# Thirty-two unused bytes ahead of the modulation columns, in a two-block forward pass on one core

## The reference

```python
# first block, twice (layer 0: short convolution; layer 1: latent attention, 8 heads)
x = layer_norm(ALPHA * x + mixer(x))            # mixer: projections, conv or attention, projection back
x = layer_norm(ALPHA * x + square(relu(x @ w1)) @ w2)      # w1: 1024 x 4096, w2: 4096 x 1024
# second block, twice (layer 0: gated linear recurrence; layer 1: block attention)
shift, scale, gate = split(silu(c) @ mod_w + mod_b, 3)
h = rms_norm(x) * (1 + scale) + shift
x = x + gate * mixer(h)
return rms_norm(x)
```

## Time and profile before

| what | value |
|---|---|
| median of 3 runs | 780.79 us (780.48, 780.79 and one of 935.18) |
| span of the profiled execution, first to last instruction | 778.4 us |
| TensorE matmuls in it | 4982, busy 768.9 us |
| VectorE, ScalarE, GpSimd busy | 586.1, 405.1 and 34.6 us |
| TensorE clock granted, mean over the span | 0.998 of full speed |
| read from memory | 172.10 MB, 222 GB/s over the span |

### The profile page before, as it was taken

The page is one execution under the profiler, slowest core; times in us unless marked ns, Lnnn a source line. Parts: engine busy times, 40 slices in busy tenths (PEclk is TensorE's granted clock), DMA queues, the critical chain, the costliest instruction groups (busy, mean ns, idle before and its releaser), DMA issues.

```text
span 778.4 us, 12084 instructions
## 1 busy us (share of the span) xinstructions
PE 768.9 (99%) x4982; PEld 697.1 (90%) x4982; DVE 586.1 (75%) x786; ACT 405.1 (52%) x512; POOL 34.6 (4%) x66
## 2 busy tenths in 40 slices
PE   9999999999999999999999999999999999999996
PEld 9999888988998889888889988998799988999995
DVE  5886898868688697687989776676687877756754
ACT  5455235545445424875355444445649869664632
POOL 0000000000000001000000000000500051000001
PEclk9999999999999999999999999999999999999999
DMA  9877438897867731446488977876235254754102
GB/s 351 319 274 278 184 125 324 348 320 289 313 231 288 290 122 62 163 139 267 165 326 344 347 273 275 308 263 245 103 109 216 109 216 163 270 216 164 55 3 80
DMA packets 26983, 173.94 MB, mean 223 GB/s; under 512 B 3248, under 2 KB 3632, under 8 KB 7856
## 3 DMA queue, kind: packets, MB, share of 16 engines
q1 hardware_dynamic: 26640, 173.14, 60.0%
q10 hardware_dynamic: 288, 0.02, 0.0%
HBM read 172.10 MB, written 1.05 MB: 222 GB/s over the span
## 4 chain that ended last, share of the span: by engine, by line
PE 93%; DVE 3%; ACT 2%; POOL 1%; issue 0%; POOLq 0%; ACTq 0%
PE bank L578 12%; PE bank L580 12%; PE bank L579 12%; PE Y L714 10%; PE Y L716 10%; PE Y L713 10%; PE bank L1067 2%; PE bank L1068 2%; PE bank L1069 2%; PE bank L996 2%; DVE w_low L1610 1%; PE bank L816 1%; PE Y L738 1%; PE bank L610 1%; PE bank L619 1%; PE bank L611 1%
## 5 line engine op out<-in xcount | busy, mean ns | idle before, releaser
L1610 DVE TENSOR_TENSOR w_low<-raw,w_high 128x2048 fp32r<-128x2048 f32 (+3 forms) x125 | 278.5, 2238 | 65.1 <-ACT w_high L1203 62.8
L1203 ACT CAST w_high<-raw 128x2048 fp32r<-128x2048 f32 (+3 forms) x125 | 232.5, 1869 | 92.9 <-DMA raw<-weights 80.0
L578 PE MATMUL bank<-xT_h,w_high 128*128 128x256 f32 x728 | 206.5, 284 | 0.1
L579 PE MATMUL bank<-xT_l,w_high 128*128 128x256 f32 x728 | 205.8, 283 | 0.0
L580 PE MATMUL bank<-xT_h,w_low 128*128 128x256 f32 x728 | 205.8, 283 | 0.0
L578 PEld LDWEIGHTS bank<-xT_h,w_high 128*128 128x128 f32 x728 | 139.4, 192 | 1.6 <-DVE w_low L1610 0.3
L579 PEld LDWEIGHTS bank<-xT_l,w_high 128*128 128x128 f32 x728 | 139.4, 191 | 1.1
L580 PEld LDWEIGHTS bank<-xT_h,w_low 128*128 128x128 f32 x728 | 139.5, 192 | 0.0
L714 PE MATMUL Y<-w_low,hT_h 128*128 128x512 f32 x324 | 128.3, 396 | 0.0
L713 PE MATMUL Y<-w_high,hT_h 128*128 128x512 f32 x324 | 128.0, 395 | 0.0
L716 PE MATMUL Y<-w_high,hT_l 128*128 128x512 f32 x324 | 101.9, 395 | 0.0
(11 more groups left out here) (291 smaller groups left out, 1144.5 us busy)
## 6 DMA issues: line engine op xcount, KB each, us to landing
raw<-weights SPq DMA_DIRECT2D x149, 1024.0 KB, 5.0
rows<-rows_in SPq DMA_DIRECT2D x9, 512.0 KB, 7.7
raw<-weights SPq DMA_DIRECT2D x4, 576.0 KB, 3.5
z<-gates_in SPq DMA_DIRECT2D x4, 512.0 KB, 3.8
raw<-weights SPq DMA_DIRECT2D x2, 896.0 KB, 4.4
raw<-weights SPq DMA_DIRECT2D x3, 512.0 KB, 7.0
x<-x_in SPq DMA_DIRECT2D x2, 512.0 KB, 4.4
kT<-rows_in SPq DMA_DIRECT2D x2, 512.0 KB, 8.3
```

Of the source, the lines that this page charges most:

```text
L578: mm(dst, high, xh[:, kt, :], start=kt == 0, stop=False)
L579: mm(dst, high, xl[:, kt, :], start=False, stop=False)
L1203: nc.scalar.copy(w_high[:, n % RING, start:COLS[n]], raw[:, s % RAW, start:COLS[n]]).then_inc(w_high_ready, 1)
L1610: tt(w_low[:, n % RING, start:COLS[n]], slot[:, start:COLS[n]], f32(w_high[:, n % RING, start:COLS[n]]), ALU.subtract).then_inc(raw_done, 1)
```

## The change

One tile of 128 x 8 float32 (32 bytes in each partition) is declared between `cols` and `modcol`. Nothing reads or writes it. No instruction is added, removed or moved; nine tiles move up by 32 bytes: `modcol`, `buf_a`, `buf_b`, `hT_h`, `hT_l`, `kT`, `area`, `small` and `prm`. `hT_h` then starts at byte 197,440, 64 past a multiple of 128, and `hT_l` at 203,584, the same.

```diff
@@ -294,6 +294,7 @@
         consts = sb("consts", [P, 2 * P + 2 * SEQ])
         ones = sb("ones", [P, P])
         cols = sb("cols", [P, NCOL])
+        sb("space_0", [P, 8])
         modcol = sb("modcol", [P, 2 * NMOD])
         buf_a = sb("buf_a", [P, 2, 512])
         buf_b = sb("buf_b", [P, 2, 512])
```

## The result

The changed kernel takes 774.95 us (median of 5 runs, 774.49 to 775.68), the kernel before 780.49 (median of 5 runs, one of which took 935.18). The ratio is 0.9931, with a 95% interval of 0.9918 to 0.9943: 5.5 us faster, and clear of noise, though well under 2%. The profiled execution took 774.49 us, the least of the five, and its span is 772.7; before it was 778.4. One unused line moves every line number behind it up by one: L713, L714, L716 of before are L714, L715, L717 here.

What follows compares the result with a forecast made beforehand. TensorE, busy for 768.9 of 778.4 us, was taken to bound the kernel. The span of 778.4 less 6.6 plus 0.8 gives 772.6, and with 2.4 us outside it 775.0; 8-in-10 range 773.2 to 781.6 us.

Steps and rivals of the forecast that it cites:

- What bounds the kernel: Whole kernel: TensorE, busy 768.9 of 778.4 us, waits for nothing long; distances between matmul starts make the time.
- What is removed: 996 matmuls with hT stationary, in down and the latents' values: each start 6.7 ns earlier, 6.6 us saved.
- the low end of 5.7: The same 996 matmuls with hT stationary, judged by record durations: 5.7 ns each, 5.7 us saved.
- second rival: Lines longer than 64 bytes make hT's new place worse: 6.6 us slower, 787.4 us, or 788 with hT moving; chance 0.07.
- What the moving side adds: 444 matmuls in mo and mla with hT moving: 0.8 us slower if the 3 and 1 ns are the address's.
- The tiles set at nothing: The other moved tiles, such as area, kT and buf_b, on TensorE, ScalarE and VectorE: no gain.
- The bound for the chain's parts on other engines: VectorE's and ScalarE's 3% and 2% of the chain: a few ns an instruction, below 0.1 us.
- First rival: The 32 bytes aren't the cause of the 6.7 ns, so no change: 780.8 us, or 781.6 with hT moving; chance 0.16.
- The rule of on-chip memory in lines of 16 bytes: Old and new hT addresses are multiples of 16, so the address change would do nothing; objection to the forecast.
- the fetch in whole lines: Fetching hT as stationary operand loses the line's part ahead of the tile: 32 bytes cost 6.7 ns a matmul.
- my reading of the 6.7 ns: hT's extra per matmul over xT as 8 lost elements at 0.83 ns, suggesting a 64-byte line.
- Third rival: Only half of hT's stationary excess is the address: 3.0 us less 0.8 won, 778.6 us; chance 0.05.

Runs made afterwards that it cites:

- the fastest kernel: Against the kernel before, padding puts xT 192 bytes, hT_h 0 and hT_l 192 from the weights' start, modulo 256: 765.57 us, ratio 0.9807.
- At 0: Against the kernel before, 96 unused bytes behind cols in place of the change's 32, so hT, like xT, is 0 from the weights modulo 256: 776.16 us.
- both at 192: Against the changed kernel, xT also moved, so xT and hT start 192 bytes from the weights' start modulo 256: 765.68 us, ratio 0.9818.

## Why the prediction was right, and where it wasn't

The predicted 775.0 us was met, within 0.1, and the mechanism was right in kind: the address of `hT` sets the distances on a full TensorE. That the number is so close is luck. Two of its terms were off in opposite directions, by 2.5 and 2.0 us, and 0.6 us more came from a start that the change isn't shown to touch. There was a fourth error: the median run has 1.8 us outside its span (774.95 to 773.2), not the 2.4 that the prediction added, and its span is 0.5 us longer than that of the profiled execution.

- What bounds the kernel: right. TensorE is busy for 99% after as before, and its waits are as few; new is one of 0.2 us for `x` at the start. The gain in a step (5.60 + 5.74 to 5.50 + 5.76) reached the end undiminished. No supply of weights came due, not even in the fastest kernel, whose step is 10.99 us and whose only wait for weights is one of 0.2 us, as before. The clock "at the top level throughout" was read from a row that doesn't show the slow distances of the first 26 matmuls.
- "What is removed", 6.6 us: mis-sized, 4.1 measured, and below the low end of 5.7. The step that failed is the one that took `xT` as the model of a tile at 64 past a multiple of 128. It isn't: `hT` went from 233.3 to 229.0 ns and not to 226.7. (The matmuls are 1002 and not 996; six in mo were overlooked, worth 0.03 us.) The second rival had named that gap and drawn the wrong conclusion from it.
- "What the moving side adds", 0.8 us: the wrong sign, 1.2 us won. I had the rows for it and read them as saying that a misaligned moving tile is a little faster and an aligned one as slow as `xT`. At 0 it is so (1.9 us more than in the changed kernel, 0.7 more than before); r = 192 is a third case.
- The tiles set at nothing: right within 0.9 us. The bound for the chain's parts on other engines was worked out too small: VectorE's 3% of the chain is 23 us, some 34 instructions, and 7 ns off each would be 0.2 us and not "below 0.1". The 0.6 us at the start had no term.
- First rival, no change: fell, by the kernel that moves only `hT`. Its point that plain float32 doesn't show the effect stays true: `kT` by `z` has records of 379 ns in all 14 traces, and starts 216 ns apart. The rule of on-chip memory in lines of 16 bytes (the Trainium skill, "SBUF — State Buffer", section "Specifications (TRN2)") doesn't decide here: every place tried is a multiple of 32, hence of 16, and `hT` stationary goes from 227 to 234 ns.
- Second rival, a line of 128: fell. So did the fetch in whole lines on which it and my reading of the 6.7 ns rested: moving the weights alone, from a multiple of 128 to 64 past one, made the matmuls with `xT` moving faster, and a lost part of a line could only have made them slower.
- Third rival, half: on the stationary side nearer than I gave it, which won 4.3 of 6.7 ns, though not by one line of `down` and not the other: by the starts L713 and L716 won 3.3 and 4.5 ns and L714 5.4. Its time, 778.6 us, was 3.7 off.
- That 2%, 15.6 us, is about what a measurement of this kernel can tell from no change: wrong. The interval of the ratio is 0.0013 to either side, 1 us, and 5.5 us stood clear of it.

## What to carry to other kernels

On a full TensorE look at the distances between starts, not at durations, and compare one line of code on two tiles: a pair like the earlier trace rows showed a gain that no wait and no busy share shows. What counted here is the distance between the starts of the moving and the stationary float32r operand modulo 256, not an alignment. For 256 moving columns of activations 192 above the weights was best, and for 512 moving columns of weights 0 was. 288 bytes of padding in all (both at 192) were worth 1.8%, because they served the most frequent matmul, the 2400 with `xT` moving. No other kernel was tried, so these places are to be measured anew elsewhere. A padding shifts every tile behind it, so state each tile's place again after each edit: the kernel with `xT` up by 64 lost its gain to that. And set apart what happens before the first real matmul: here it varied by more than 1 us from trace to trace, as much as some of the effects looked for.

## What was not expected of the hardware

- Float32r matmuls with a full weight load before each start 113.5 to 120 ns apart for 256 columns, and 226.7 to 234 for 512, depending on the distance between their operands' starts modulo 256. The records of weight loads hardly tell: 187 to 189 ns on `hT` in `down` in all 14 kernels, and in `up` a mean of 192 before and 188 in the fastest kernel.
- At r = 192, with 256 columns, there are two rates, 113.5 and 117.8 ns, that hold for whole stretches of one program. They may also differ between executions, as the times of 765.2 to 768.3 us suggest. Which of them is taken depends on a tile that the stretch doesn't touch. What decides it, and the mechanism behind the distances, stay open.
- The matmuls of 128 columns at the start went from 213 to some 110 ns apart between 3.9 and some 7 us from the span's start, in another place in nearly every trace; the first record of the clock at full speed stands there.
